# Hybrid decoder layer on one core: value products one slot later, score masks and weight splits ahead of the scan on VectorE

## Chip, core and metric

One core of a Trainium2 chip (trn2). The metric is the device time of one launch in microseconds (us), lower is better. All arithmetic is fp32; each large product is made of three passes in a reduced fp32 form.

## What is computed

One inference step of a one-layer hybrid decoder, for 256 prompt tokens and 8 sequences of 8 new tokens (320 tokens, model width 2048). Cut to what matters:

```python
z = rmsnorm(x) @ w_in                       # 2048 -> 5120
q, k, v, u, h, gb, gc = split(z)            # three mixers read z
o_att = dilated window attention(q, k, v)   # 16 heads of 64; sequences read 1280 of the 2048 cached rows each
y_ssm = complex diagonal scan over time(u), then GELU and a gated linear unit
y_conv = gb * conv3(gc * h)
mixed = concat(rmsnorm(o_att), rmsnorm(y_ssm), rmsnorm(y_conv))
x = x + mixed @ w_out
x = x + (silu(xn @ w_gate) * (xn @ w_up)) @ w_down
y = rmsnorm(x)
```

## The kernel before

**Tiles.** Features lie on the 128 partitions, the 320 tokens on the free axis. A weight *unit* is 128x1024 numbers (512 KB): two input tiles of 128 by 512 outputs. ScalarE (ACT) rounds a unit to its high part (`high`, L581, tile `whi`), VectorE (DVE) subtracts to get the low part (`low`, L886, `wlo`), and TensorE (PE) runs 24 matmuls of 320 columns on it (L1724 to L1726: high by high, high by low, low by high). `whi` and `wlo` have two buffers, so unit s+2 is split after PE has finished unit s and before it begins unit s+2.

**Slots.** The program up to the last third of the output projection is written as 96 slots. In slot s, PE runs unit s; `middle(s)` puts other matmuls after half of its unit, `end(s)` puts more behind it. Units 0 to 79 are the input projection, 80 and later the output projection. Each engine has its own hand-written order over the slots, and constants say which slot holds what:

- `START_OF[b]` is the first slot of sequence b; the sequences are six slots apart. In steps 0 to 4 PE makes the scores (`scores`, L1532) and DVE masks them out of bank 6 (`mask_scores`, L919); in step 4 ACT takes the exponent (L604); in step 5 PE turns the first two pieces of the probabilities (L1551), in step 6 the third, and ACT copies them out (L612); in steps 6 to 10 PE multiplies by the cached values (`values`, L1558), and in step 11 turns the result (L1581). Sequences 0 and 1 are finished late, in `LATE_SLOTS`.
- The scan runs over 16 groups of states, five parts each (`scan`, L936 to L958), all on DVE, spread over slots 24 to 65. Before a group, PE projects it in a `middle` (L1505, banks 6 and 7) and ACT copies it out (L687); GpSimd (POOL) makes the table of the group's powers. Part 0 of a group waits for both.
- The attention of the prompt runs over 8 pairs of heads from slot `PROMPT0`: scores (L1590), masks on DVE (L975), exponents, `prompt_norms` on DVE (L986), turning on PE (L1605), product (L1616).
- Three of the five norms lie in the slots: the input norm (its sum on PE in slot 8, its chain on DVE in slots 9 and 10: L853, L857 to L859), that of the scan's output (`SUM_SSM`: sum L1488, root on ACT, chain, `normed` L991) and that of the convolution (`SUM_CONV`).
- In DVE's slot come, in this order: two evictions (in every eighth slot, later every second), variance, `prompt_norms`, `prompt_masks`, those scan parts up to the last part 0 of the slot, two evictions, `mask_scores`, `low(s + 2)`, other work, and the remaining scan parts.

**Transfers.** All are issued by the SyncE queue (SP), in program order: the unit five slots ahead, then the cache pieces (512 KB each) of the slot. Each score step takes two pieces, each value step two; they share a ring of `KV` = 7 buffers, and a piece is issued when the one seven places ahead of it has been used.

**After the slots** PE runs the rest of the output projection and the feed-forward layer in loops (L1779 to L1781, L1828 to L1830), where nothing is changed. At the end the squares of the last tiles are added, the scale is spread over the partitions, DVE scales 12 output tiles (L1262) and POOL four (L1477), two tiles at a time, and SP stores them.

## Time and profile before

| | us |
|---|---|
| median of 3 runs | 1553.22 (1550.26 to 1553.37) |
| the profiled execution | 1552.25 |
| its span, first to last instruction | 1550.4 |
| PE busy | 1508.8 |
| DVE busy | 818.3 |
| ACT busy | 572.4 |
| POOL busy | 266.2 |

The profiled execution is 1.0 us under the median, and its span 1.85 us under its own time. PE is busy in the records when any matmul runs; a matmul's record is longer than the distance to the next one. The granted TensorE clock is 0.993 of full speed on average over the span.

### The profile page before, as it was taken

What the parts mean: (1) busy time and instruction counts of PE and PEld (TensorE: products, weight loads), DVE (VectorE), ACT (ScalarE), POOL (GpSimd) and SP (SyncE); (2) the same over time, 40 slices, a digit from 0 to 9 for tenths busy, and PEclk for the clock granted to TensorE, in tenths of its full rate; (3) what the DMA queues carried; (4) which work ended last, traced back from release to release, by engine and by line L of the source; (5) the groups of instructions that cost most, each with busy time, mean ns of one, the idle gap of its engine ahead of it and who ended that gap; (6) DMA issues with size and microseconds to landing.
All of it is one profiled execution on the core that took longest, in us unless ns stands there. A gap on an engine that the chain in (4) does not pass through costs nothing.

```text
span 1550.4 us, 27086 instructions
## 1 busy us (share of the span) xinstructions
PE 1508.8 (97%) x11084; PEld 1422.2 (92%) x11084; DVE 818.3 (53%) x1063; ACT 572.4 (37%) x751; POOL 266.2 (17%) x371
## 2 busy tenths in 40 slices
PE   9999999999989999999999999999999999999997
PEld 8998777667777899999999999999999999999997
DVE  6668987674264767544444444444444433333334
ACT  6333332225554435333333333333333333333332
POOL 7986655420170000000000000000000000000100
PEclk9999999999999999999999999999999999999998
DMA  7545799989669544444444444444444444444442
GB/s 257 186 158 196 258 361 349 360 321 343 249 230 391 165 139 149 149 150 149 149 149 149 149 149 149 149 148 150 149 148 150 148 150 150 150 148 152 148 151 107
DMA packets 82994, 296.59 MB, mean 191 GB/s; under 512 B 9952, under 2 KB 10848, under 8 KB 82528
## 3 DMA queue, kind: packets, MB, share of 16 engines
q1 hardware_dynamic: 82912, 295.43, 55.8%
q8 instruction: 60, 0.98, 0.3%
q14 instruction: 22, 0.18, 0.0%
HBM read 289.31 MB, written 5.43 MB: 190 GB/s over the span
## 4 chain that ended last, share of the span: by engine, by line
PE 82%; DVE 6%; issue 6%; DMA 4%; ACT 1%; POOL 1%; SPq 0%; POOLq 0%; ACTq 0%; DVEq 0%
PE ps L1829 18%; PE ps L1828 18%; PE ps L1830 18%; PE ps L1724 6%; PE ps L1726 5%; PE ps L1725 5%; DMA kv<-in_cv 3%; PE ps L1532 2%; PE ps L1558 2%; DVE wlo L886 1%; PE ps L1781 1%; PE ps L1780 1%; PE ps L1779 1%; DVE tm L937 1%; PE ps L1505 1%
## 5 line engine op out<-in xcount | busy, mean ns | idle before, releaser
L1151 DVE TENSOR_TENSOR wlo<-raw,whi 128x1024 fp32r<-128x1024 f32 x264 | 325.2, 1232 | 519.9 <-ACT whi L768 519.8
L768 ACT ACTIVATE whi<-raw 128x1024 fp32r<-128x1024 f32 x264 | 279.9, 1060 | 606.2 <-PE ps L1830 601.7
L1830 PE MATMUL ps<-xh,wlo 128*128 128x320 f32 x1400 | 432.8, 309 | 0.0
L1828 PE MATMUL ps<-xh,whi 128*128 128x320 f32 x1400 | 432.8, 309 | 0.0
L1829 PE MATMUL ps<-xl,whi 128*128 128x320 f32 x1400 | 432.7, 309 | 0.0
L1828 PEld LDWEIGHTS ps<-xh,whi 128*128 128x128 f32 x1400 | 262.8, 188 | 0.0
L1829 PEld LDWEIGHTS ps<-xl,whi 128*128 128x128 f32 x1400 | 262.8, 188 | 0.0
L1830 PEld LDWEIGHTS ps<-xh,wlo 128*128 128x128 f32 x1400 | 262.8, 188 | 0.0
L1724 PE MATMUL ps<-xh,whi 128*128 128x320 f32 x760 | 246.1, 324 | 9.2 <-DVE wlo L886 6.1
L1726 PE MATMUL ps<-xh,wlo 128*128 128x320 f32 x760 | 235.8, 310 | 0.0
L1725 PE MATMUL ps<-xl,whi 128*128 128x320 f32 x760 | 235.7, 310 | 0.0
L1830 PE MATMUL ps<-hh,wlo 128*128 128x320 f32 x696 | 215.2, 309 | 0.0
L1828 PE MATMUL ps<-hh,whi 128*128 128x320 f32 x696 | 215.2, 309 | 0.0
L1829 PE MATMUL ps<-hl,whi 128*128 128x320 f32 x696 | 215.1, 309 | 0.0
L581 ACT ACTIVATE whi<-raw 128x1024 fp32r<-128x1024 f32 x111 | 117.5, 1059 | 242.6 <-PE ps L1726 213.6
L886 DVE TENSOR_TENSOR wlo<-raw,whi 128x1024 fp32r<-128x1024 f32 x111 | 143.3, 1292 | 88.7 <-ACT whi L581 88.5
L1468 POOL TENSOR_TENSOR sq_last<-sq_last 128x1280 f32<-128x1280 f32 x2 | 5.9, 2970 | 1006.2 <-ACT sq_last L562 1006.2
L1724 PEld LDWEIGHTS ps<-xh,whi 128*128 128x128 f32 x760 | 143.6, 189 | 35.5 <-issue 25.7
L1725 PEld LDWEIGHTS ps<-xl,whi 128*128 128x128 f32 x760 | 143.8, 189 | 0.6
L1726 PEld LDWEIGHTS ps<-xh,wlo 128*128 128x128 f32 x760 | 143.6, 189 | 0.0
L1830 PEld LDWEIGHTS ps<-hh,wlo 128*128 128x128 f32 x696 | 130.7, 188 | 0.0
L1829 PEld LDWEIGHTS ps<-hl,whi 128*128 128x128 f32 x696 | 130.7, 188 | 0.0
(301 smaller groups left out, 1502.9 us busy)
## 6 DMA issues: line engine op xcount, KB each, us to landing
raw<-in_w_gu SPq DMA_DIRECT2D x176, 512.0 KB, 3.4
raw<-in_w_dn SPq DMA_DIRECT2D x88, 512.0 KB, 3.4
kv<-in_ck SPq DMA_DIRECT2D x80, 512.0 KB, 7.6
kv<-in_cv SPq DMA_DIRECT2D x80, 512.0 KB, 7.8
raw<-in_w_in SPq DMA_DIRECT2D x79, 512.0 KB, 4.9
raw<-in_w_out SPq DMA_DIRECT2D x32, 512.0 KB, 3.5
out_kv<-z SPq DMA_DIRECT2D x2, 1280.0 KB, 9.9
x<-in_xt SPq DMA_DIRECT2D x4, 640.0 KB, 9.8
```

The costliest lines, as they stand in the source:

```text
L581: act.activation(whi[:, u % SPL, :], raw[:, u % RAW, :], ACT.Copy).then_inc(S["w_hi"], 1)
L768: act.activation(whi[:, j % SPL, :], raw[:, j % RAW, :], ACT.Copy).then_inc(S["w_hi"], 1)
L886: v.tensor_tensor(wlo[:, u % SPL, :], raw[:, u % RAW, :], whi[:, u % SPL, :].bitcast(F32), ALU.subtract) \
L1151: v.tensor_tensor(wlo[:, j % SPL, :], raw[:, j % RAW, :], whi[:, j % SPL, :].bitcast(F32), ALU.subtract) \
L1532: last = t_.matmul(ps[32 * c:32 * c + 32, 6, cols], qst[:, b % 2, 2 * c + half, :], keys(2 * c + half), start=(half == 0), stop=(half == 1 ...
L1558: last = t_.matmul(ps[32 * c:32 * c + 32, bank, 0:2 * P], turned[:, 32 * c:32 * c + 32], vals[:, 2 * P * c:2 * P * c + 2 * P], start=start ...
L1724: t_.matmul(out, whi[:, u % SPL, w], xh[:, k, :], start=first, stop=False)
L1725: t_.matmul(out, whi[:, u % SPL, w], xl[:, k, :], start=False, stop=False)
L1726: last = t_.matmul(out, wlo[:, u % SPL, w], xh[:, k, :], start=False, stop=final)
L1828: t_.matmul(out, whi[:, slot, w], ah[:, k, :], start=(k == 0), stop=False)
L1829: t_.matmul(out, whi[:, slot, w], al[:, k, :], start=False, stop=False)
L1830: last = t_.matmul(out, wlo[:, slot, w], ah[:, k, :], start=False, stop=(k == 2 * units - 1))
```

## The change

- `START_OF` begins one slot earlier for every sequence. Scores, exponents and turned probabilities come a slot earlier; the value products are now steps 7 to 11, so they keep their slots, and the result is turned in step 12, also the same slot. In `end(s)` PE makes values before it turns probabilities. The pieces in the ring are ordered accordingly: two in the first score slot, four in each of the next four, two in the slot of the last values.
- On DVE no scan part stands ahead of the late evictions, masks and split any more: all parts of a slot come last. The 62 later parts are spread over 28 slots instead of 29.
- The prompt's attention, the gated unit and the norm of the scan's output come one slot earlier; the late products of sequences 0 and 1 in slots 57 and 61 instead of 58 and 60.
- The input norm's chain takes slots 9, 10 and 11, and the evictions behind it slots 12 to 14. The scan norm's chain takes two slots.
- DVE adds the four tiles of squares of the second and third norm in two operations, and PE makes one matmul of the sum instead of four.
- The first two x tiles and the first weight unit are loaded whole. Four reloads of x are issued apart instead of two by two.
- The output is scaled in nine pieces, the first two on DVE of one tile.

```diff
-LATE_SLOTS = (58, 60)
+LATE_SLOTS = (57, 61)
-SCAN0, SCAN1, SCAN_END, SCAN_FIRST = 24, 37, 66, 18
-PROMPT0 = 67
-SUM_SSM, SUM_CONV = 77, 84
+SCAN0, SCAN1, SCAN_END, SCAN_FIRST = 24, 37, 65, 18
+PROMPT0 = 66
+SUM_SSM, SUM_CONV = 76, 84
-START_OF = (37, 43, 49, 55, 61, 67, 73, 79)
+START_OF = (36, 42, 48, 54, 60, 66, 72, 78)
+TURN, VALUES, OUTPUT = 5, 7, 12
-SAMPLE_SLOT = START_OF[-1] + 12
+SAMPLE_SLOT = START_OF[-1] + OUTPUT + 1
...
+        Y_DVE = ((4, 1), (5, 1), (6, 2), (8, 2), (10, 2), (12, 2), (14, 2))
+        Y_POOL = ((0, 2), (2, 2))
...
-            here += [("v", b, j, 0) for b in range(DEC_BATCH) for j in range(KEY_TILES) if START_OF[b] + 6 + j // 2 == s]
+            here += [("v", b, j, 0) for b in range(DEC_BATCH) for j in range(KEY_TILES) if START_OF[b] + VALUES + j // 2 == s]
...
                 if s == N_IN:
...
-                    for c in range(2):
-                        sy.dma_start(x1[:, 4 * c:4 * c + 4, :], a["xt"][:, 4 * c:4 * c + 4, :]).then_inc(S[f"x_back{c}"], 16)
+                    load_x(0)
+                if s == N_IN + 2:
+                    load_x(1)
...
-            for kk in range(2):
-                sy.dma_start(x1[:, kk, :], a["xt"][:, kk, :]).then_inc(S[("x_first", "x_in0")[kk]], 16)
-                half = slice(512 * kk, 512 * kk + 512)
-                sy.dma_start(raw[:, 0, half], weight(0)[:, half]).then_inc((S["raw_first"], RAW_IN[0])[kk], 16)
-            for j in range(1, U_IN):
+            for j in range(U_IN):
                 sy.dma_start(x1[:, 2 * j:2 * j + 2, :], a["xt"][:, 2 * j:2 * j + 2, :]).then_inc(S[f"x_in{j}"], 16)
                 if j < RAW:
                     unit(j)
...
-                parts = scan_parts(s)
-                starts = [n for n, (_, part) in enumerate(parts) if part == 0]
-                early_parts = starts[-1] + 1 if starts else 0
-                for i, part in parts[:early_parts]:
-                    scan(i, part)
                 if is_last(s) and s >= 2 * U_IN - 1:
                     evict(s, 2)
                     evict(s, 3)
...
                 if s == 10:
-                    scales_rest(0, rstd)
+                    rstd_step(v.tensor_tensor(rtmp[:], rstd[:], rstd[:], ALU.mult))
+                if s == 11:
...
-                if 11 <= s < 15:
-                    evict(U_IN - 1, s - 11)
+                if s in (12, 13, 14):
+                    for n in ((0,), (1,), (2, 3))[s - 12]:
+                        evict(U_IN - 1, n)
...
+                for n, (at, src) in enumerate(((SUM_SSM - 1, sqs), (SUM_CONV - 1, sqc))):
+                    if s == at:
+                        dve.wait_ge(S["sq_ready"], 5 + n)
+                        step(v.tensor_tensor(src[:, 0:2], src[:, 2:4], src[:, 0:2], ALU.add))
+                        v.tensor_tensor(src[:, 0], src[:, 1], src[:, 0], ALU.add).then_inc(S["sq_paired"], 1)
...
                 if s == SUM_SSM:
-                    scales(1, rstd_s)
+                    scales_first(1, rstd_s)
+                if s == SUM_SSM + 1:
+                    scales_rest(1, rstd_s)
                     normed(ZU, V_OUT + 12, rstd_s)
-                for i, part in parts[early_parts:]:
+                for i, part in scan_parts(s):
                     scan(i, part)
...
-                    sums(sqs, range(NC), 5)
+                    sums(sqs, [0], 5)
...
-                for b in batches(s, 5):
-                    turn_probabilities(b, 0)
-                    turn_probabilities(b, 1)
                 for step in range(KN):
                     for b in batches(s, step):
                         scores(b, step)
-                for step in range(6, 11):
-                    for b in batches(s, step):
-                        values(b, 2 * step - 12)
-                        values(b, 2 * step - 11)
+                for j in range(0, KEY_TILES, 2):
+                    for b in batches(s, VALUES + j // 2):
+                        values(b, j)
+                        values(b, j + 1)
+                for b in batches(s, TURN):
+                    turn_probabilities(b, 0)
+                    turn_probabilities(b, 1)
```

The order that results, at three places. **DVE in slots 26 and 27** (`tm` and `hb` are scan tiles, `wlo` the split; before, lines L886 and L936; now L892 and L942), before:

```order
L886 TENSOR_TENSOR wlo<-raw,whi 128x1024
L949 TENSOR_TENSOR tm<-tm,tab 128x640
L950 TENSOR_TENSOR tm<-tm,tab 128x640
L955 TENSOR_TENSOR hb<-tm 128x320
L956 TENSOR_TENSOR hb<-tm 128x320
L958 COPY ho<-hb 128x2x9
L936 TENSOR_TENSOR tm<-xs,tab 128x640
L937 TENSOR_TENSOR tm<-xs,tab 128x640
L886 TENSOR_TENSOR wlo<-raw,whi 128x1024 x2
```

Now:

```order
L892 TENSOR_TENSOR wlo<-raw,whi 128x1024
L955 TENSOR_TENSOR tm<-tm,tab 128x640
L956 TENSOR_TENSOR tm<-tm,tab 128x640
L961 TENSOR_TENSOR hb<-tm 128x320
L962 TENSOR_TENSOR hb<-tm 128x320
L964 COPY ho<-hb 128x2x9
L892 TENSOR_TENSOR wlo<-raw,whi 128x1024
L942 TENSOR_TENSOR tm<-xs,tab 128x640
L943 TENSOR_TENSOR tm<-xs,tab 128x640
```

The split of unit 29 stood behind part 0 of the next group and now stands ahead of it.

**DVE in slots 55 and 56**, from the four evictions of slot 55 to the mask of slot 56, on which PE's turning of the new values in slot 56 waits. Before, the split stands behind a mask (not shown), and nine scan operations follow it:

```order
L886 TENSOR_TENSOR wlo<-raw,whi 128x1024
L945 SCALAR_TENSOR_TENSOR tm<-dec,tm 128x320
L946 SCALAR_TENSOR_TENSOR tm<-dec,tm 128x320
L949 TENSOR_TENSOR tm<-tm,tab 128x640
L950 TENSOR_TENSOR tm<-tm,tab 128x640
L955 TENSOR_TENSOR hb_odd<-tm 128x320
L956 TENSOR_TENSOR hb_odd<-tm 128x320
L958 COPY ho<-hb_odd 128x2x9
L936 TENSOR_TENSOR tm<-xs,tab 128x640
L937 TENSOR_TENSOR tm<-xs,tab 128x640
L919 ISA sall,smax<-ps,mask 128x256
```

Now:

```order
L892 TENSOR_TENSOR wlo<-raw,whi 128x1024
L955 TENSOR_TENSOR tm<-tm,tab 128x640
L956 TENSOR_TENSOR tm<-tm,tab 128x640
L961 TENSOR_TENSOR hb_odd<-tm 128x320
L962 TENSOR_TENSOR hb_odd<-tm 128x320
L964 COPY ho<-hb_odd 128x2x9
L942 TENSOR_TENSOR tm<-xs,tab 128x640
L943 TENSOR_TENSOR tm<-xs,tab 128x640
L925 ISA sall,smax<-ps,mask 128x256
```

Seven scan operations stand between that split and that mask instead of nine; the two of part 2 (L951, L952) have moved ahead of the evictions.

**DVE around the second norm** (`rstd_s` is its scale, `sp` the prompt's probabilities, which PE waits for at L1605), before:

```order
L886 TENSOR_TENSOR wlo<-raw,whi 128x1024
L853 RECIPROCAL rstd_s<-rtmp 128x320
L857 TENSOR_TENSOR rtmp<-rstd_s 128x320
L858 SCALAR_TENSOR_TENSOR rtmp<-rtmp,var 128x320
L859 SCALAR_TENSOR_TENSOR rstd_s<-rtmp,rstd_s 128x320
L991 SCALAR_TENSOR_TENSOR z<-z,vec,rstd_s 128x320 x4
L982 RECIPROCAL pmax<-pmax 128x4
L986 TENSOR_SCALAR sp<-sp,pmax 128x128
```

Now:

```order
L859 RECIPROCAL rstd_s<-rtmp 128x320
L988 RECIPROCAL pmax<-pmax 128x4
L992 TENSOR_SCALAR sp<-sp,pmax 128x128
L992 TENSOR_SCALAR sp<-sp,pmax 128x256
L992 TENSOR_SCALAR sp<-sp,pmax 128x128
L992 TENSOR_SCALAR sp<-sp,pmax 128x256
L892 TENSOR_TENSOR wlo<-raw,whi 128x1024
L1113 RECIPROCAL rsum<-rsum 128x1
L863 TENSOR_TENSOR rtmp<-rstd_s 128x320
L864 SCALAR_TENSOR_TENSOR rtmp<-rtmp,var 128x320
L865 SCALAR_TENSOR_TENSOR rstd_s<-rtmp,rstd_s 128x320
L997 SCALAR_TENSOR_TENSOR z<-z,vec,rstd_s 128x320 x4
```

Only the reciprocal is left ahead of the prompt's norms; three steps and four multiplications stand behind them and behind the split.

## Rows read from the trace of the kernel before

**Rows 1.** The page's line of busy time by engine

```profile
PE 1508.8 (97%) x11084; PEld 1422.2 (92%) x11084; DVE 818.3 (53%) x1063; ACT 572.4 (37%) x751; POOL 266.2 (17%) x371
```

**Rows 2.** Windows: start:end, length, busy us per engine, PEclk, DMA share, GB/s

```profile
100.00:155.00 55.00, 51.48 (x337) 47.18 (x336) 46.60 (x59) 16.98 (x20) 35.31 (x36) 1.00 0.58 191
...
185.00:225.00 40.00, 38.51 (x359) 28.38 (x358) 35.31 (x61) 12.41 (x20) 27.20 (x27) 1.00 0.89 345
...
225.00:265.00 40.00, 36.98 (x353) 28.65 (x352) 28.25 (x51) 11.60 (x19) 19.51 (x19) 1.00 0.90 336
...
700.00:1500.00 800.00, 800.00 (x5456) 800.00 (x5455) 338.96 (x270) 273.35 (x264) 9.25 (x4) 1.00 0.46 149
```

**Rows 3.** Waits of PE over the whole span: total us, times, longest

```profile
PE ps L1558 <- DMA kv<-in_cv: 8.2, 8, 1.9
...
PE ps L1724 <- DVE wlo L886: 6.1, 4, 1.7
...
PE ps L1558 <- ACT ptk L612: 1.7, 1, 1.7
...
PE ps L1605 <- ACT ptk L612: 1.3, 1, 1.3
...
PE ps L1505 <- DVE smax L919: 1.0, 2, 0.5
...
PE ps L1551 <- ACT sall L604: 0.9, 1, 0.9
...
PE ps L1532 <- DVE pmax L975: 0.8, 1, 0.8
```

**Rows 4.** Timeline of PE: start, us, line, [idle before it <- releaser]

```profile
12.43 0.42 PE L1724 MATMUL ps<-xh,whi 128*128 128x320 f32 x1 [1.40 <-DVE wlo L886]
...
57.50 0.42 PE L1724 MATMUL ps<-xh,whi 128*128 128x320 f32 x1 [1.70 <-DVE wlo L886]
...
118.32 0.41 PE L1724 MATMUL ps<-xh,whi 128*128 128x320 f32 x1 [1.50 <-DVE wlo L886]
...
280.71 0.39 PE L1685 MATMUL ps<-ident,z 128*64 128x128 f32 x1 [2.41 <-DVE smax L919]
...
452.22 0.47 PE L1605 MATMUL ps<-ident,sp 128*128 128x128 f32 x1 [3.01 <-DVE sp L986]
...
506.63 0.39 PE L1724 MATMUL ps<-xh,whi 128*128 128x320 f32 x1 [1.30 <-issue]
```

**Rows 5.** Timeline of DVE, two pieces from 115 to 120 us

```profile
115.46 1.24 DVE L937 TENSOR_TENSOR tm<-xs,tab 128x640 f32<-128x640 f32 x1
...
116.63 3.20 DVE L886 TENSOR_TENSOR wlo<-raw,whi 128x1024 fp32r<-128x1024 f32 x2
```

**Rows 6.** Groups of DVE instructions: busy, mean ns | idle before

```profile
L945 DVE TENSOR_TENSOR_SCAN tm<-dec,tm 128x320 f32<-128x320 f32 x16 | 14.2, 885 | 0.5 <-DVE tm L942 0.2
```

**Rows 7.** Timeline of DVE: first norm's last step, and the split behind it

```profile
54.00 1.22 DVE L859 SCALAR_TENSOR_TENSOR rstd<-rtmp,rstd 128x320 f32<-128x320 f32 x1
...
55.26 2.19 DVE L886 TENSOR_TENSOR wlo<-raw,whi 128x1024 fp32r<-128x1024 f32 x1
```

**Rows 8.** Windows behind the gaps at 280.71 and 452.22

```profile
280.50:284.00 3.50, 3.29 (x15) 3.07 (x16) 1.28 (x3) 1.18 (x2) 3.42 (x7) 0.52 1.00 421
...
452.30:459.00 6.70, 6.70 (x31) 6.02 (x32) 3.43 (x9) 1.88 (x7) 5.46 (x10) 0.58 0.23 78
```

**Rows 9.** Timeline of PE: the second norm's sum, 4 matmuls of 2 passes

```profile
435.52 2.42 PE L1488 MATMUL ps<-sqs,ones 128*128 128x320 f32 x8
```

**Rows 10.** Timeline of ACT: the second half of the first weight unit

```profile
7.60 0.63 ACT L665 ACTIVATE whi<-raw 128x512 fp32r<-128x512 f32 x1 [1.07 <-DMA raw<-in_w_in]
```

**Rows 11.** Windows: a stretch of cache loads; the tail

```profile
246.00:253.00 7.00, 5.28 (x56) 4.29 (x56) 5.38 (x9) 1.06 (x1) 6.92 (x8) 1.00 1.03 411
...
1541.00:1550.40 9.40, 1.24 (x6) 1.05 (x5) 4.48 (x6) 0.44 (x1) 3.03 (x2) 0.50 0.73 279
```

**Rows 12.** DMA issues: KB each, median us from issue to landing

```profile
out_y<-yout SPq DMA_DIRECT2D x8, 320.0 KB, 2.6
```

79 lines of the change are left out of this document (42 added, 37 removed).

## Prediction, made before the changed kernel was run

> **What bounds it now.** I read the page's busy line first: TensorE is busy for 1508.8 of 1550.4 us [rows 1], so only what shortens or closes up its work counts. The table of windows says where: from 700 to 1500 us it is busy in all 800.00 us, while windows before 351 us miss 1.5 to 3.5 us each [rows 2]. The change leaves the loops alone, so whatever is won in the slots arrives whole at the end. Third, the waits of TensorE and the single gaps [rows 3, 4]: that is the list to be worked through. In the scan's stretch DVE is busy for 46.60 of 55 us [rows 2], close to a bound of its own. Fourth, the granted clock: behind the gaps of 2.41 and 3.01 us it is 0.52 for 3.50 us and 0.58 for 6.70 us [rows 8], a mix of the levels of 1.2 and 2.4 GHz. TensorE had stood still before both falls.
>
> **Startup: 1.5 us.** Unit 1 starts at 12.43 after 1.40 us of waiting [rows 4]; the second half of the first weight is there only for a copy at 7.60 [rows 10]. The same bytes now come in two transfers instead of four and SP issues two less. The first product must then wait for the whole unit, about where that copy starts. Nothing saved to 2.0 us; I take 1.5, since unit 1 waits longer than one copy.
>
> **First norm: 1.3 us.** Its three steps ran in one piece, the last 1.22 us, and the split behind them 2.19 us [rows 7]; TensorE waited 1.70 us at 57.50 [rows 4]. Now one step stands in slot 10, two in 11. Two steps of 1.22 beside a split that itself ran for up to 2.19 just exceed what a slot leaves, so 0.4 us may stay. Bounds 1.2 and 1.7.
>
> **Scan ahead of the split: 2.0 us.** Waits for `wlo` are 6.1 us in four [rows 3]: 1.40, 1.70, and 3.0 in two gaps like that at 118.32 [rows 4]. Part 0 of a group stood ahead of the split; its second operation alone took 1.24 us, and two splits followed it back to back [rows 5]. It now stands behind. But DVE does the same work in 46.60 of 55 us [rows 2]: at the eviction slots 31 and 39, TensorE arrives earlier at a bank that DVE has not emptied, and gives about 1 us back. Bounds 1.0 and 3.0. Projections wait 1.0 us for masks [rows 3]; masks go earlier where no third scan part is in the way: 0.5 us.
>
> **Cache pieces: 5.6 us.** Eight waits, 8.2 us [rows 3]. A slot with scores and values asks for five pieces, 2.62 MB, five slots running; now four slots running, with two lighter slots beside them. At the 411 GB/s of the stretch 246 to 253 us [rows 11], 2.62 MB take 6.4 us, near a slot's own time there, so the backlog grows with each slot, and a shorter run with a rest before it cuts the later waits. Two thirds of 8.2 go: 5.6. Bounds 2, if only one wait in four was the last of such a run, and 8.2.
> A rule speaks against this: the Trainium skill (DMA: Bandwidth & Descriptors, Bandwidth) puts the limit of HBM traffic of one core at about 358 GB/s. By it the stretch from 185 to 265 us, at 345 and 336 GB/s [rows 2], would already be at its limit, and this term would be about 2 instead of 5.6. The trace shows 411 [rows 11], above it, so I go by the trace; the case is part of the second rival.
>
> **The new values at 280.71: 0.9 and 1.7 us.** They wait 2.41 us for the mask of slot 56 [rows 4]. Nine scan operations stood ahead of that mask, seven now; the two that leave take about 2 x 0.85 us (a scan operation is 885 ns on average [rows 6]), and TensorE also arrives earlier, so about 1.5 us of wait stay. Then the clock should not fall: 3.50 us at 0.52 cost 3.50 x 0.48 = 1.7 us [rows 8]. Bounds for both together 0 and 4.1.
>
> **Late product: 1.7 us.** Sequence 1's late product shared slot 60 and bank 7 with turned probabilities and waited 1.7 us for ACT's copy [rows 3]. In slot 61 bank 7 has long been emptied. Bounds 1.2 and 1.7.
>
> **Second norm: 2.6 and 2.8 us.** PE waited 0.9 us for the exponent [rows 3] and 3.01 us for `sp` behind the whole chain [rows 4]. Now values cover the exponent, and only the reciprocal is ahead of `sp`. What is late next is bank 6: turned probabilities and the prompt's still meet in slot 77, as where 1.3 us were waited for ACT's copy [rows 3]. So 0.9 + 3.0 - 1.3 = 2.6. The clock at 0.58 for 6.70 us cost 2.8 us [rows 8]; 1.3 us is no gap behind which it fell. Bounds 3 and 6.7. The steps now follow in slot 77, behind its split; the next split is a whole slot away, which hides them. If DVE were late there, the masks of pair 6 would be next.
>
> **Sums: 3.2 us.** Four matmuls of two passes take 2.42 us [rows 9], the last pass some 0.2 us of overhang; three quarters of 2.2 go, 1.6 us, twice. DVE's four added operations lie in slots 75 and 83, where no scan is left. Bounds 2.8 and 3.6.
>
> **Smaller ones.** Prompt masks late by 0.8 us [rows 3] stood behind an eviction that waited for reloaded x; one reload is issued later, 0.6 us. At 506.63 TensorE waited 1.30 us [rows 4] for evictions behind the third norm's chain; this chain is whole still, one more operation of the attention follows it, and TensorE comes earlier by what its sum no longer takes, so 0.7 us *more*. Bounds -1.5 and 0. Tail: stores run at 279 GB/s over 9.40 us [rows 11], so they end earlier only as the first starts earlier; half of one two-tile multiplication (4.48 / 6 / 2) gives 0.4 us. The Trainium skill (the same page and section) lets transfers of 64 KB move at 138 and of 1 MB at 341 GB/s, so that splitting a 320 KB store costs rather than gives; by that the tail would be 0.2 us longer and the whole sum 0.6 less. Here 320 KB land in 2.6 us amid other stores [rows 12]; the term is too small for either to matter to the range.
>
> **Sum.** 1.5 + 1.3 + 2.0 + 0.5 + 5.6 + 0.9 + 1.7 + 1.7 + 2.6 + 2.8 + 3.2 + 0.6 - 0.7 + 0.4 = 24.1 us. Every engine's order is new over 60 slots, so waits that no row shows will appear; I allow three of 0.9 us, the size of the exponent's wait [rows 3]: 2.7. That leaves 21.4. The profiled execution, 1552.25, would become 1530.9; against the median of 1553.2, 1531.8.
>
> **Rivals.**
> *More is given back (0.30).* DVE and the transfers bound the scan's stage: no gain for splits, projections and the mask at 280.71 (2.0, 0.5, 0.9), 2 instead of 5.6 for the cache, the clock falls again there (1.7) and new waits take 3 more. That is 11.7 less: 1543.5. For it: 46.60 of 55 us on DVE and 345 GB/s [rows 2]. Against: DVE's busy share falls to 28.25 of 40 us later, and 411 GB/s.
> *All of it closes up (0.10).* No new waits, all cache waits and splits gone: 2.7 + 2.6 + 1.0 more, and 1 at the start: 1524.5.
> *The scan falls behind (0.05), slower.* With all parts last, part 0 of a group is done late in its slot; ACT must see it before it may copy the next projection out, and the high part of unit s+2 is queued behind that copy, and the split and TensorE behind it. It decides once DVE is later than a slot's second half plus the projection, some 3 us. If 13 groups of slots 37 to 65 then each wait for one part 0, about 2 us (0.9, a scan operation's mean [rows 6], and 1.24 [rows 5]), that is 26 us: 1558. Against: the windows from 185 to 265 us hold some six slots each, and DVE is busy in them for 35.31 and 28.25 us of 40 [rows 2].
> *It does not arrive (0.05).* The gaps closed in the slots open again before evictions, whose order is unchanged, as a bank can be taken only when DVE has emptied it: 1553, within 0.2%, which is about what a measurement of this kernel can tell from no change (3.1 us).
>
> **Numbers.** The forecast has 0.50 (1526 to 1538), the others as said. Faster by over 0.2%: 0.50 + 0.30 + 0.10 = 0.90; same 0.05; slower 0.05. The likeliest is 1531.8. The range reaches down to the third case, 1524.0, and up past the second's 1543.5, whose new waits may be larger by half, to 1546.0; outside lie the last two cases and the ends of these, under 2 in 10.
>
> **What would show it.** In the new profile: no wait of TensorE over 2 us in the slots, no window at a clock near 0.5 before the tail, two passes at the sums, DMA waits for values under 3 us in total, nothing over 0.5 us at the end of slots 12, 28 and 35, and a wait of about 2 us before slot 86. The start of the loops should be some 21 us earlier. Wrong would be: waits for `xs` or `wlo` at many slots from 37 to 65 (the slower rival), or the saving shrinking between slot 43 and slot 66 (the first).

## The result, and the profile after

| | before | after |
|---|---|---|
| median | 1553.3 us (1550.26 to 1554.12, 4 runs) | 1536.14 us (1534.52 to 1537.62, 4 runs) |
| the profiled execution | 1552.25 | 1536.85 |
| its span | 1550.4 | 1535.0 |
| granted TensorE clock, mean | 0.993 | 0.996 |

The ratio is 0.9893, 95% interval 0.9876 to 0.991: 16.6 us faster by this ratio, with 14.0 to 19.3 us inside the interval. The forecast was 21.4 us less (1531.8, range 1524.0 to 1546.0). Three executions further down, two of the kernel before and one of the old slot numbers, took 2455 us or more in a disturbed state, and all medians are taken without them.

The page's busy line of the changed kernel, beside [rows 1]:

```profile
PE 1504.5 (98%) x11072; PEld 1417.8 (92%) x11072; DVE 824.9 (54%) x1068; ACT 572.1 (37%) x751; POOL 264.6 (17%) x371
```

TensorE is busy for 4.3 us less. The rest of the 15.4 us between the spans was idle time.

The waits of PE over the whole span of the changed kernel (total us, times, longest), beside [rows 3]:

```profile
PE ps L1571 <- DMA kv<-in_cv: 5.3, 5, 2.1
PE ps L1737 <- issue: 3.5, 2, 2.7
PE ps L1737 <- DVE z L908: 2.7, 3, 1.4
PE ps L1618 <- DVE smax L925: 1.9, 1, 1.9
...
PE ps L1698 <- DVE smax L925: 1.7, 1, 1.7
PE ps L1564 <- ACT xs L693: 1.5, 1, 1.5
...
PE ps L1545 <- ACT xs L693: 0.9, 1, 0.9
PE ps L1737 <- DVE wlo L892: 0.9, 2, 0.7
PE ps L1618 <- ACT ptk L619: 0.8, 2, 0.4
```

Waits for `wlo` fell from 6.1 to 0.9 us, waits for `ptk` from 3.0 to 0.8, and those for `sp`, `sall` and `pmax` are gone. Cached values fell only from 8.2 to 5.3. Waits for late evictions (`z`, L908) grew from 0.5 to 2.7. Three kinds are new: for `xs` (2.4 us in two), for a score mask in front of the prompt's turning (L1618, 1.9 us), and a longer one at the output projection's eviction (L1737 <- issue).

The gaps one by one, from the timeline of PE of the changed kernel, beside [rows 4]:

```profile
107.64 0.41 PE L1737 MATMUL ps<-xh,whi 128*128 128x320 f32 x1 [0.72 <-DVE wlo L892]
...
127.85 0.38 PE L1737 MATMUL ps<-xh,whi 128*128 128x320 f32 x1 [1.42 <-DVE z L908]
...
177.93 0.74 PE L1564 MATMUL ps<-ident,sall 128*128 128x128 f32 x5 [1.46 <-ACT xs L693]
...
275.83 1.03 PE L1698 MATMUL ps<-ident,z 128*64 128x128 f32 x8 [1.67 <-DVE smax L925]
...
450.25 0.85 PE L1618 MATMUL ps<-ident,sp 128*128 128x128 f32 x6 [1.86 <-DVE smax L925]
...
490.31 0.38 PE L1737 MATMUL ps<-xh,whi 128*128 128x320 f32 x1 [2.67 <-issue]
```

The gap at 280.71 of before is the one at 275.83 here (2.41 to 1.67 us), that at 506.63 is now at 490.31 (1.30 to 2.67). The last two gaps stand behind these pieces of DVE's timeline, first slot 79, then slots 85 and 86:

```profile
447.29 0.87 DVE L908 TENSOR_TENSOR z<-ps,rstd 128x320 f32<-128x320 f32 x2
448.08 1.68 DVE L1004 TENSOR_TENSOR xl<-z,xh 128x320 fp32r<-128x320 f32 x4
449.69 0.41 DVE L925 CUSTOM_DVE_ANT_0 sall<-ps,mask 128x256 f32<-128x256 f32 x1
...
485.55 2.15 DVE L859 RECIPROCAL rstd<-rtmp 128x320 f32<-128x320 f32 x1 [0.56 <-ACT rtmp L573]
487.74 0.49 DVE L863 TENSOR_TENSOR rtmp<-rstd 128x320 f32<-128x320 f32 x1
488.26 0.49 DVE L864 SCALAR_TENSOR_TENSOR rtmp<-rtmp,var 128x320 f32<-128x320 f32 x1
488.79 0.49 DVE L865 SCALAR_TENSOR_TENSOR rstd<-rtmp,rstd 128x320 f32<-128x320 f32 x1
489.32 0.48 DVE L1009 SCALAR_TENSOR_TENSOR al<-z,vec,ah 128x256 fp32r<-128x256 f32 x1
489.72 1.68 DVE L913 TENSOR_TENSOR x<-ps,x 128x320 f32<-128x320 f32 x4
```

In slot 79 two evictions and four low parts of the gated tiles (L1004, `mixed_low`) stand ahead of the mask (L925) that clears bank 6, a bank of PSUM that TensorE needs next. In slot 86 the evictions stand behind 3.6 us of chain (2.15 + 3 x 0.49) and 0.48 of the attention.

The windows of the changed kernel (start:end, length, busy us per engine, PEclk, DMA share, GB/s), beside [rows 2, 8]:

```profile
185.00:225.00 40.00, 39.38 (x366) 29.55 (x365) 34.35 (x61) 12.45 (x20) 24.24 (x27) 1.00 0.92 346
225.00:265.00 40.00, 37.87 (x354) 28.27 (x353) 30.79 (x52) 12.44 (x20) 22.67 (x26) 1.00 0.91 341
...
491.00:494.70 3.70, 3.70 (x17) 3.70 (x17) 3.70 (x7) 0.00 (x0) 0.00 (x0) 0.54 0.55 187
700.00:1500.00 800.00, 800.00 (x5456) 800.00 (x5456) 338.66 (x269) 273.48 (x264) 9.26 (x4) 1.00 0.46 149
```

The loops are as they were. The two stretches at half clock [rows 8] are gone, and a new one stands behind the gap of slot 86; at 0.54 for 3.70 us it cost 3.70 x 0.46 = 1.7 us by the clock (1.3 to 1.5 by the time of its stage, as the last section shows).

By stages, from the first matmul of each slot in the two traces (us between them):

| stage | before | after | gain |
|---|---|---|---|
| start to slot 1 | 12.4 | 11.1 | 1.3 |
| slots 1 to 14 | 48.7 | 47.0 | 1.7 |
| slots 14 to 36 | 87.6 | 86.2 | 1.4 |
| slots 36 to 66 | 197.6 | 194.9 | 2.7 |
| slots 66 to 76 | 80.0 | 80.4 | -0.4 |
| slots 76 to 80 | 37.1 | 31.5 | 5.6 |
| slots 80 to 86 | 43.2 | 39.2 | 4.0 |
| slots 86 to 95 | 38.7 | 40.1 | -1.4 |
| slot 95 to the end | 1005.1 | 1004.7 | 0.4 |

The steps of the sequences lie one slot earlier, so the work of a stage is not quite the same in both. Still, the missing part is plain: for slots 36 to 66 the terms of the forecast came to 10.4 us (0.5 + 5.6 + 0.9 + 1.7 + 1.7), and 2.7 came.

The prediction had named signs to look for. Seen as named: two passes at the sums, and nothing over 0.5 us at the end of slots 12, 28 and 35. Not seen as named: TensorE waited over 2 us twice (2.67 in front of slot 86, where about 2 had been named, and 2.07 for a cached piece), one stretch near half clock came ahead of the tail, waits for values were 5.3 us instead of under 3, and the loops begin 14.9 us earlier instead of some 21. Of the two signs that it would be wrong, the saving did not shrink between slots 43 and 66 (2.3 us at slot 43, 7.1 at slot 66), and waits for `xs` came at two slots, not at many.

### The profile page after: what moved, and what is told of

Its sections match the earlier page's. It is cut to its first block, busy times and chain, and to the rows that moved or that the text cites. A ratio compares the mean times of both kernels' runs of the same rounds, so it can differ in the third digit from the quotient of the medians.

```text
span 1535.0 us, 27068 instructions
## 1 busy us (share of the span) xinstructions
PE 1504.5 (98%) x11072; PEld 1417.8 (92%) x11072; DVE 824.9 (54%) x1068; ACT 572.1 (37%) x751; POOL 264.6 (17%) x371
## 4 chain that ended last, share of the span: by engine, by line
PE 85%; DVE 6%; issue 5%; DMA 2%; ACT 1%; POOL 1%; POOLq 0%; ACTq 0%; DVEq 0%
PE ps L1842 19%; PE ps L1841 19%; PE ps L1843 19%; PE ps L1737 6%; PE ps L1739 6%; PE ps L1738 6%; DMA kv<-in_cv 2%; PE ps L1545 2%; PE ps L1571 2%; DVE wlo L892 1%; PE ps L1794 1%; PE ps L1793 1%; PE ps L1792 1%; PE ps L1637 1%; PE ps L1532 1%
## 5 line engine op out<-in xcount | busy, mean ns | idle before, releaser
L1737 PE MATMUL ps<-xh,whi 128*128 128x320 f32 x760 | 245.6, 323 | 7.1 <-issue 3.5
L892 DVE TENSOR_TENSOR wlo<-raw,whi 128x1024 fp32r<-128x1024 f32 x111 | 142.4, 1283 | 79.8 <-ACT whi L588 79.4
L1737 PEld LDWEIGHTS ps<-xh,whi 128*128 128x128 f32 x760 | 143.2, 188 | 32.4 <-issue 29.6
L1841 PEld LDWEIGHTS ps<-hh,whi 128*128 128x128 f32 x696 | 130.6, 188 | 0.0
```

The source lines that it names most:

```text
L892: v.tensor_tensor(wlo[:, u % SPL, :], raw[:, u % RAW, :], whi[:, u % SPL, :].bitcast(F32), ALU.subtract) \
L1737: t_.matmul(out, whi[:, u % SPL, w], xh[:, k, :], start=first, stop=False)
L1841: t_.matmul(out, whi[:, slot, w], ah[:, k, :], start=(k == 0), stop=False)
```

## Experiments

Each is the changed kernel with one edit, unless said otherwise. Old slot numbers, scan early, third norm spread and mask first ran on one chip (before: 1550.4 us there); these two together, four sums, short values and second norm whole on another (1549.2); the changed kernel again, the old slot numbers again, half units and five places mended on a third (1550.5). Since cached pieces come later or earlier from one execution to the next, and stretches at half clock come and go, the trace is read beside the times in one table (all from the profiled execution; "falls" are the stretches at half clock ahead of the tail, with their lengths in us):

| kernel | median, us | ratio, 95% | slot 95 begins | waits for cached values | slot 95 less these | falls |
|---|---|---|---|---|---|---|
| before | 1553.3 | 1 | 545.3 | 8.2 | 537.1 | 3.4, 6.8 |
| after | 1536.1 | 0.9893 [0.9876, 0.991] | 530.4 | 5.3 | 525.1 | 3.4 |
| after, again | 1534.9 | 0.9902 [0.9885, 0.9919] | 527.8 | 2.8 | 525.0 | 3.4 |
| old slot numbers | 1538.8 | 0.993 [0.9913, 0.9946] | 528.0 | 5.4 | 522.6 | 3.4 |
| the same, again | 1540.4 | 0.9927 [0.9904, 0.995] | 535.8 | 7.7 | 528.1 | 3.4, 3.4, 3.4 |
| scan early | 1536.3 | 0.9913 [0.9894, 0.9931] | 529.7 | 3.6 | 526.1 | 3.4 |
| third norm spread | 1532.5 | 0.9887 [0.9871, 0.9904] | 524.5 | 2.7 | 521.8 | none |
| mask first | 1533.2 | 0.9887 [0.9871, 0.9904] | 527.6 | 2.4 | 525.2 | 6.8 |
| these two | 1531.9 | 0.9889 [0.9874, 0.9905] | 524.8 | 4.0 | 520.8 | none |
| four sums | 1536.4 | 0.9915 [0.9901, 0.9929] | 531.6 | 4.1 | 527.5 | 3.4 |
| short values | 1531.0 | 0.9881 [0.9866, 0.9897] | 524.7 | 0 | 524.7 | 3.4 |
| second norm whole | 1537.7 | 0.9924 [0.991, 0.9939] | 534.7 | 5.8 | 528.9 | 3.4, 3.4 |
| half units | 1536.7 | 0.9911 [0.9895, 0.9927] | 529.9 | 2.6 | 527.3 | 6.8 |
| five places mended | 1527.4 | 0.9853 [0.9834, 0.9872] | 521.3 | 3.3 | 518.0 | none |

The column "less these" agrees to 0.1 us between the two executions of the changed kernel, whose slot 95 began 2.6 us apart. That is closer than it can be trusted: single stages of the two still differ by up to 0.6 us and happen to cancel, and the two executions of the old slot numbers differ by 5.5 in this column, of which the two further stretches at half clock explain 3.4. Differences of single edits are therefore read from the stage that the edit touches. The ratios cannot carry them alone: those of third norm, mask first and both (0.9887 to 0.9889) lie 0.6 to 2.3 us under the two of the changed kernel (0.9893 and 0.9902), well inside each other's intervals.

**The slot numbers.** All parts of the change stay, in the old slots:

```diff
-LATE_SLOTS = (57, 61)
+LATE_SLOTS = (58, 60)
-SCAN0, SCAN1, SCAN_END, SCAN_FIRST = 24, 37, 65, 18
-PROMPT0 = 66
-SUM_SSM, SUM_CONV = 76, 84
+SCAN0, SCAN1, SCAN_END, SCAN_FIRST = 24, 37, 66, 18
+PROMPT0 = 67
+SUM_SSM, SUM_CONV = 77, 84
-START_OF = (36, 42, 48, 54, 60, 66, 72, 78)
-TURN, VALUES, OUTPUT = 5, 7, 12
+START_OF = (37, 43, 49, 55, 61, 67, 73, 79)
+TURN, VALUES, OUTPUT = 5, 6, 11
```

> The changed kernel with the slot numbers of the kernel before (values in steps 6 to 10, scan end, prompt, second norm and late products back in their slots); the orders inside a slot, the two norm chains, the paired sums, startup and tail stay changed. Theory A (each closed gap is won by its own part of the change): the numbers carry the late product (1.7 us) and the shorter cache waits (8.2 to 5.3, so 2.9 us), but also cost the 1.4 us longer gap before slot 86 and its fall of the clock (1.7 us), so this kernel takes 1537 to 1540 us, waits for cache pieces come back to about 8 us and no clock near 0.5 is seen in the slots. Theory B (the numbers carry nearly all, the order inside the slots nothing): 1546 us or more.

Measured 1538.79 us (1535.19 to 1540.93), ratio 0.993: slower than the changed kernel, as the first theory said, but not in the way it said: in this profile the waits for cached values were 5.4 us, not 8, and a stretch at half clock was there (at 439.5 us) that it had ruled out. So it was run once more, beside the changed kernel.

> The changed kernel itself, unchanged, on the same chip and against the same runs of the kernel before as the next three. Its ratio was 0.9893 [0.9876, 0.991]. Theory A (ratios of different chips can be compared to 0.1%): 0.988 to 0.9905, 16 to 17 us saved. Theory B (the kernel before differs from chip to chip by the luck of its cache loads, and the ratio moves with it): outside of that.

1534.91 us (1533.89 to 1537.49), ratio 0.9902: the ratios on the two chips agree to 0.1%, as the first theory had it, though 15.2 us saved are a little under its 16 to 17.

> The changed kernel with the old slot numbers once more (sequences, prompt, scan end, norm and late products where they were, the order of values and turned probabilities and all other parts as changed), beside the changed kernel on one chip. Theory A (the new slot numbers are worth what the first ratios say, 0.993 against 0.9893): 4 to 7 us slower than the changed kernel, mainly by longer waits for cached values. Theory B (they are worth what the two profiles say, in which slot 95 began at 528.0 with the old numbers and at 530.4 us with the new): within 2 us of the changed kernel, so that the gain comes from the order inside the slots, the norms, the sums and the start.

1540.40 us is the median (1536.24 to 1543.10): 5.5 us slower than the changed kernel, ratio 0.9927 against 0.9902. The first theory holds, though the two intervals overlap a little (0.9904 to 0.995, and 0.9885 to 0.9919); the first pair of ratios says the same. From the waits of PE and its timeline in this run:

```profile
PE ps L1571 <- DMA kv<-in_cv: 7.7, 7, 2.9
...
286.34 0.64 PE L1571 MATMUL ps<-kv,ptk 128*32 128x256 f32 x8 [2.95 <-DMA kv<-in_cv]
```

And the three stretches at half clock that are in it, as windows:

```profile
250.20:253.60 3.40, 3.40 (x15) 2.35 (x15) 2.58 (x3) 0.00 (x0) 2.54 (x4) 0.50 1.03 412
287.70:291.20 3.50, 3.50 (x15) 2.24 (x15) 0.00 (x0) 0.00 (x0) 1.03 (x1) 0.51 1.03 408
311.60:315.00 3.40, 3.40 (x15) 3.40 (x15) 2.30 (x5) 0.00 (x0) 1.09 (x2) 0.51 0.33 117
```

Two of them follow a late cached piece (2.95 us at 286.34, 1.91 us at 248.86) and one the late product, which waits 1.69 us for `ptk` again. In the three profiles with the old numbers (before among them) cached values are waited for 8.2, 5.4 and 7.7 us, mean 7.1. In the ten with the new numbers and whole pieces it is 2.4 to 5.8, mean 3.7. So the new numbers take off some 3.4 us of waiting and, in some executions, the falls behind it. But with the old numbers slot 86 waited 1.30 instead of 2.67 us and the mask of slot 79 not at all: the new numbers brought both of these. The edit puts the late products back with the sequences, so it does not tell their shares apart.

**Scan parts ahead of masks and split again.**

```diff
+                parts = scan_parts(s)
+                starts = [n for n, (_, part) in enumerate(parts) if part == 0]
+                early_parts = starts[-1] + 1 if starts else 0
+                for i, part in parts[:early_parts]:
+                    scan(i, part)
                 if is_last(s) and s >= 2 * U_IN - 1:
...
-                for i, part in scan_parts(s):
+                for i, part in parts[early_parts:]:
```

> The changed kernel with the scan parts up to the last part 0 of a slot again ahead of the late evictions, masks and split. Theory A: the gaps of 1.5 us for splits before slots 29 and 36 and the long wait for the mask in slot 56 (over 2.4 us, with the clock down for 3.4 us) come back, 5.4 us, and the waits for the copy of a projection in slots 41 and 61 (1.46 and 0.89 us) and some of the other new ones go, so 1538 to 1540 us. Theory B (DVE's work bounds the stage, so its order only moves the gaps): 1535 to 1537 us, and slot 66 starts within 1 us of the changed kernel's.

1536.28 us (1534.89 to 1539.46), and 526.1 against 525.0 in the table: the second theory's time holds, and the first's 1538 to 1540 does not. From the timeline of PE of this kernel, the old waits are back and one is new:

```profile
116.92 0.42 PE L1742 MATMUL ps<-xh,whi 128*128 128x320 f32 x1 [1.78 <-DVE wlo L892]
...
147.34 0.41 PE L1742 MATMUL ps<-xh,whi 128*128 128x320 f32 x1 [1.49 <-DVE wlo L892]
...
273.77 0.41 PE L1742 MATMUL ps<-xh,whi 128*128 128x320 f32 x1 [2.56 <-DVE z L908]
```

Slots 14 to 36 take 88.9 us here against 86.2 and 86.6 in the two executions of the changed kernel, so there the new order is worth 2.3 to 2.7. Slots 36 to 66, less their waits for cached values, take 188.4 against 190.4 and 189.8: there it costs 1.4 to 2.0, because the waits for `xs` come with it. The order is a gain in the first half of the scan and a loss in the second. The reason that the second theory gave, that DVE's work bounds the stage, is not what this shows: the last experiment below does the same work in less time.

**The third norm's chain spread over two slots.**

```diff
                 if s == SUM_CONV:
-                    scales(2)
+                    scales_first(2)
                 if s == SUM_CONV + 1:
+                    scales_rest(2, rstd)
                     normed(ZH, V_OUT, rstd)
```

> The changed kernel with the third norm's chain spread as the second's: only the reciprocal in its slot, the three steps in the next one behind the split. Theory A (the gap of 2.67 us before slot 86 is this chain ahead of the evictions, and the clock fell because of it): the gap shrinks to 1 us or less, the clock stays up, 1532 to 1533 us. Rival (the chain is only late somewhere else: the normed tiles, and PE waits for them at slot 88): 1536 us, with a new gap of about 2 us at slot 88.

1532.54 us (1531.67 to 1533.58), and 3.2 us less in the table. The timeline of PE has

```profile
485.71 0.38 PE L1738 MATMUL ps<-xh,whi 128*128 128x320 f32 x1 [1.09 <-issue]
```

and no stretch at half clock in the slots. Slots 80 to 86 take 37.6 us instead of 39.2, slots 86 to 95 take 38.8 instead of 40.1: 1.6 us of gap and 1.3 of clock, as the first theory had it.

**The mask of slot 79 ahead of the low parts.**

```diff
-                if s == N_IN - 1:
-                    mixed_low(ZU, 12, KT)
                 for step_ in range(KN):
                     for b in batches(s, step_):
                         mask_scores(b, step_)
+                if s == N_IN - 1:
+                    mixed_low(ZU, 12, KT)
```

> The changed kernel with the score mask of slot 79 ahead of the four low parts of the scan's output. Theory A (the 1.86 us before the prompt's turning in slot 79 is the mask behind these four): the gap goes, 1534 to 1534.5 us. Rival (cache pieces or the reloads of x bound the next slots): the 1.86 us come back as waits for transfers by slot 83, 1536 us.

1533.16 us (1532.48 to 1534.02). The gap of 1.86 us is gone, and slots 76 to 80 take 29.9 us instead of 31.5. But the stretch at half clock behind the gap of slot 86 was 6.8 us long in this profile instead of 3.4 (slots 86 to 95 take 41.3 instead of 40.1), and slot 1 began 0.6 us later, so the table shows nothing (525.2). Both edits together:

> The changed kernel with two edits together: the third norm's chain spread over slots 84 and 85, and in slot 79 the mask of the last sequence's scores ahead of the four low parts of the gated tiles. Theory A (gaps are independent, and each stands on what DVE has in line ahead of the operation that TensorE waits for): the wait of 1.86 us at slot 79 and about 1.6 of the 2.67 us at slot 86 go, together with the stretch at half clock that cost 1.7 us; in the slots no granted clock near 0.5 is left; span 4 to 5.5 us under that of the changed kernel, 1530.5 to 1532. Theory B (an engine that is freed at one place gives it back at the next): the two edits together give no more than the larger alone, 1532.5 to 1534.

1531.91 us (1530.41 to 1534.04), span 1530.2. The trace is as the first theory had it: slots 76 to 80, 80 to 86 and 86 to 95 take 29.9, 37.7 and 38.8 us, each as in the run of its own edit, with no fall. The gap of 1.86 us is gone, that of slot 86 is down to 1.09. The median is only 0.6 us below that of the third norm's edit alone, on another chip, and the ratios are the same (0.9889 and 0.9887), so the times by themselves do not show that the second edit adds anything.

**The sums as four matmuls again** (L1656 and L1660 back to `sums(sqs, range(NC), 5)` and `sums(sqc, range(NC), 5)`, DVE's four additions left out).

> The changed kernel with the sums of the second and third norm made again by four matmuls over the four tiles of squares, and without DVE's four additions. Theory A (the term of the sum was right: three of four matmuls of two passes each fall away, twice): TensorE is busy 3.2 us longer and the time rises by 2.8 to 3.6 us, to 1539 to 1540. Theory B (the matmuls filled time in which TensorE would have waited for evictions or for the split): the time rises by under 1 us.

1536.35 us (1534.78 to 1538.70). TensorE is busy for 1508.4 us instead of 1504.5 and 1505.0. Timeline of PE, this kernel's sum (the changed kernel's takes 0.81 us, in two passes) and the wait of slot 79:

```profile
423.11 2.42 PE L1496 MATMUL ps<-sqs,ones 128*128 128x320 f32 x8
...
451.92 0.85 PE L1613 MATMUL ps<-ident,sp 128*128 128x128 f32 x6 [0.93 <-DVE smax L925]
```

The term is right: 2.42 - 0.81 = 1.6 us, twice. But the first 1.6 us shorten the wait for the mask of slot 79 by 0.93 (from 1.86), so the kernel loses 2.4 us by the table, between the two theories (2.0 of them in slots 76 to 86, where the sums are). In the changed kernel 0.9 of the sums' 3.2 us ran into that wait.

**Short pieces of values.** 256 of 1024 columns are loaded of each piece of cached values after the first seven, so the attention's output is computed from incomplete values:

```diff
-                sy.dma_start(kv[:, n % KV, :], src).then_inc(KV_IN[n % KV], 16)
+                if kind == "v" and n >= KV:
+                    sy.dma_start(kv[:, n % KV, 0:256], src[:, 0:256]).then_inc(KV_IN[n % KV], 16)
+                else:
+                    sy.dma_start(kv[:, n % KV, :], src).then_inc(KV_IN[n % KV], 16)
```

> The changed kernel, but the cached pieces of values after the first seven load only 256 of their 1024 columns, so part of the attention's input is left out; count and order of the transfers are the same. Theory A (what is left of the waits for cached values, 5.3 us in five, is the rate of the transfers, and nothing else stands behind it): those waits go, the time falls by 4 to 5.3 us, to 1531 to 1532. Theory B (the stage of slots 36 to 65 is bound by DVE as well, which would be late next): the waits for values go, but waits for evictions, masks or the copy of the projection take over more than half of it; the time falls by 2 us or less.

1531.04 us (1530.01 to 1531.51). By the ratio, 0.9881, that is 1.9 to 3.3 us less than the changed kernel; the 4 to 5.3 us of the first theory were counted from one profile with many such waits. No wait for values is left, the other large gaps of the stage are where they were and within 0.1 us as long, and the table gives 524.7 against 525.1 and 525.0. The windows:

```profile
185.00:225.00 40.00, 39.38 (x366) 29.52 (x366) 34.34 (x62) 12.46 (x20) 24.71 (x28) 1.00 0.73 245
225.00:265.00 40.00, 39.99 (x373) 30.70 (x373) 33.52 (x57) 12.45 (x20) 22.67 (x26) 1.00 0.81 260
```

At 245 and 260 instead of 346 and 341 GB/s, DVE does as much and is not late more often. So the waits for cached values add to the time as they stand, and DVE is not what held them up: the first theory.

**The second norm's chain in one piece, ahead of the prompt's norms.**

```diff
                 if s == SUM_SSM:
-                    scales_first(1, rstd_s)
-                if s == SUM_SSM + 1:
-                    scales_rest(1, rstd_s)
+                    scales(1, rstd_s)
                     normed(ZU, V_OUT + 12, rstd_s)
```

> The changed kernel with the second norm's chain and its four multiplications again in one piece in slot 76, ahead of the prompt's norms of that slot. Theory A (the two largest terms of the sum are due to this edit alone): TensorE waits about 2.5 to 3 us for sp at slot 77 or 78 and runs at half clock for 3.4 to 6.8 us behind it; the time rises by 4 to 5.5 us, to 1540 to 1542. Theory B (the move by one slot and the changed order of values and turned probabilities already cover the chain): the wait is under 1.5 us, no fall of the clock, the time rises by 1.5 us or less.

1537.71 us (1537.28 to 1541.83), ratio 0.9924 against 0.9893 and 0.9902: 3.4 to 4.8 us. Timeline of PE:

```profile
440.14 1.11 PE L1616 MATMUL ps<-ident,sp 128*128 128x128 f32 x4 [3.04 <-DVE sp L992]
```

A stretch of 3.4 us at half clock begins at 439.9, and the mask of slot 79 is waited for 0.93 us less: 3.0 + 1.7 - 0.9 = 3.8. Slots 76 to 80, where all of this lies, take 34.5 us instead of 31.5: 3.0, and not all of 3.8. The table also shows 528.9 - 525.1 = 3.8, but by chance: slot 1 began 1.2 us later in this profile, one more stretch at half clock stands at 286.3 behind a wait for a cached piece, and the one behind slot 86 is missing. First theory by the wait and the clock; the time rose by less than its 4 to 5.5 us.

**Start with half units** (two tiles of x and two halves of the first weight unit, each with its own transfer and semaphore, as before).

> The changed kernel with the first two x tiles and the first weight unit loaded in two halves each again, on SP, ACT and DVE as before. Theory A (the startup term of the sum): unit 1 starts at 12.4 instead of 11.1 us and the time rises by 1.3 to 1.5 us. Theory B (the first wait of unit 1 comes from the second unit's own load, which varies from run to run): unit 1 starts at 11.4 or earlier, no difference.

1536.74 us (1535.26 to 1537.49), 1.8 us slower than the changed kernel on the same chip. Unit 1 starts at 12.37 us; in the changed kernel at 11.11 and 11.67. First theory; 0.7 to 1.3 us of it are the start itself, and the stretch at half clock was 6.8 us long in this profile. The second theory is not wholly out: over the twelve profiles here with the first unit loaded whole, unit 1 starts at 11.10 to 12.34 us, 11.5 in the mean, against 12.43 and 12.37 in the two with halves. So the term is worth some 0.9 us on average, and one execution in twelve had next to nothing of it.

**Five places mended.** To the two edits above come: part 0 ahead of masks and split in slots 40 and 60 alone, the last part of group 1 in slot 31, part 0 of group 12 in slot 56.

```diff
+SCAN_LATER = {(1, 4): 31, (12, 0): 56}
...
+            if (i, part) in SCAN_LATER:
+                return SCAN_LATER[i, part]
...
+                starts = [n for n, (_, part) in enumerate(parts) if part == 0 and s in (40, 60)]
```

> The changed kernel with the third norm's chain spread, the mask of slot 79 ahead of the low parts, part 0 of the scan ahead of masks and split in slots 40 and 60 alone, the last part of group 1 in slot 31 instead of 30, and part 0 of group 12 (with its projection) one slot later, in 56. Theory A (every gap is closed by its own edit): beside the kernel with the first two edits, whose slot 95 began at 524.8 us, the waits of 1.46 us at slot 41 and 0.89 at slot 61 go, that of 1.51 at slot 32 falls under 0.8, that of 1.67 at slot 56 falls under 0.5; slot 95 begins 3 to 4.5 us earlier and the time is 1527 to 1529. Theory B (DVE is near its bound there and each of these only moves the wait): slot 66 begins within 1.5 us of where it did, 1530 to 1532.

1527.41 us (1526.42 to 1530.03), ratio 0.9853 [0.9834, 0.9872] against the kernel before, and 7.5 us less than the changed kernel on the same chip: faster than both. First theory. The waits for `xs` at slots 41 and 61 and that for the mask at slot 56 are under 0.5 us, that of slot 32 is 0.50. Two new gaps, in the timeline of PE:

```profile
174.48 0.81 PE L1527 MATMUL ps<-z,bt 32*128 32x320 f32 x4 [1.10 <-DVE smax L933]
...
473.83 0.51 PE L1510 MATMUL ps<-sqc,ones 128*128 128x320 f32 x1 [1.27 <-DVE sqc L1089]
```

The first is the price of part 0 in slot 40: its two operations, 2.1 us, now stand ahead of that mask. The second was 0.3 us; the additions stood behind evictions that waited for reloaded x, as TensorE now arrives earlier there.

## Why the forecast was right, and where it was not

**Right in size.** Startup: 1.5 forecast, 1.3 and 0.8 in the two profiles of the changed kernel, some 0.9 over all profiles. First norm: 1.3, and slots 1 to 14 gained 1.7. Late product: 1.7, gone in the new profile and back as 1.69 us with the old numbers. Second norm: 2.6 of waiting; the piece taken apart removes 3.0 of waiting, of which 0.9 came back at slot 79. Its clock: 2.8 forecast from 6.70 us at 0.58; undone, the piece brought a stretch of 3.4 us back, 1.7. Sums: 3.2 forecast, 3.2 measured on the engine, of which 0.9 is hidden in the changed kernel. Prompt masks: the 0.8 us are gone. Wait at 280.71: 0.9 forecast, 0.7 came (1.1 in the second profile), and the clock no longer falls there. Tail: 0.4 forecast, 0.4 in one profile and -0.2 in the other, too small to be told from nothing. The first norm, the late product's slot, the reloads of x and the tail were undone by no run of their own; these terms rest on the waits that are gone from the trace.

**Cache pieces: mis-sized.** The term said that two thirds of 8.2 us go, 5.6. In the profile compared, 2.9 went; over ten profiles with the new numbers the mean left is 3.7, so about 3.4 to 4.5 go. The mechanism fits: fewer pieces in a row, and less waiting in the mean; that the waits are the transfers' own is shown by the short pieces, while the backlog itself was tested by no run. What the step missed is that the wait is no fixed quantity of the kernel: the same code gave 5.3 and 2.8. The bounds of 2 and 8.2 held it. As to the limit of about 358 GB/s in the Trainium skill (DMA: Bandwidth & Descriptors, Bandwidth): two of the windows above, of the old slot numbers, run at 412 and 408. The same page, in its table of measured transfers, has one core alone at 425 GB/s for a transfer of 16 MB and calls about 358 the share of a core when both of a pair stream; this case, with one core, agrees with that.

**Slot 86: wrong in a cause and in its consequence.** The step was "0.7 us *more*" for the wait in front of it; it became 1.4 us more (1.30 to 2.67). Of its three causes the shorter sum is none. With the old slot numbers and one matmul for the sum the wait is 1.30 us as before, and with the new numbers and four matmuls it is 2.66: DVE's chain starts behind the sum and moves with it. Timelines of PE and DVE from that sum on, with the old slot numbers and then in the changed kernel:

```profile
479.50 0.70 PE L1501 MATMUL ps<-sqc,ones 128*128 128x320 f32 x2
...
487.00 1.07 PE L1571 MATMUL ps<-kv,ptk 128*32 128x256 f32 x16
...
488.78 1.68 DVE L913 TENSOR_TENSOR x<-ps,x 128x320 f32<-128x320 f32 x4
```

```profile
480.04 0.78 PE L1501 MATMUL ps<-sqc,ones 128*128 128x320 f32 x2 [0.28 <-DVE sqc L1081]
...
486.57 1.07 PE L1571 MATMUL ps<-kv,ptk 128*32 128x256 f32 x16
```

From the start of the sum the evictions begin after 9.28 us and, in the changed kernel, after 9.68 (489.72): the attention's operation costs 0.4. TensorE is through after 8.57 us and now after 7.60, as less turning of probabilities stands in slots 84 and 85 than with the old numbers: 1.0. Together these are the 1.4, and the step had the first of them but not the second. It also did not ask whether a gap of that length brings half clock, though [rows 8] showed a fall behind 2.41 us: another 1.3 to 1.7. The edit that spread this third chain takes the fall away and 1.6 us of the gap.

**The scan ahead of the split: right, and then not.** 2.0 and 0.5 us were claimed for the whole scan. Undoing it costs 2.3 to 2.7 us in slots 14 to 36 and gives 1.4 to 2.0 in slots 36 to 66. The chain that brings this was described, under the slower rival: part 0 last, ACT's copy of the next projection behind it, and its readers behind that. The rival expected the high part of the weights to be the victim, at 13 groups; it was at two places, and its victims were turned probabilities and scores, since bank 6 is not free until the copy is done. ACT's timeline at slot 41 of the changed kernel:

```profile
177.08 0.70 ACT L693 ACTIVATE xs<-ps 128x640 f32<-128x640 f32 x1 [2.24 <-DVE tm L943]
```

So that rival was right in kind and wrong by a factor of ten in its size: 26 us at 13 groups, against 2.4 us at two places.

**The allowance for new waits: too small.** Three of 0.9 us were allowed, 2.7. Late evictions and splits came at slot 27 (0.72 us), 32 (0.9 more than before), 40 (0.63) and 48 (0.62), of which the scan's term had set 1 aside; beside them 1.46 us at slot 41, 0.89 at slot 61, and 1.86 at slot 79. The largest could have been read from the order beforehand: four low parts of 0.42 us each and two evictions ahead of a mask, in a slot where the mask is now awaited, since the prompt's probabilities are turned in odd slots instead of even ones.

**The sum.** The forecast had 13.7 us of waiting less and 7.7 us less of matmuls (sums 3.2, clock 1.7 and 2.8); the traces have 11.1 and 4.3. The waiting, against the terms: cache 2.7 short, slot 86 0.7, the scan's order 1.9, new waits 1.5 beyond the allowance, the mask at 280.71 0.2, together 7.0. More than forecast went of the waits for ACT's copies of `ptk` in the prompt (1.8: two of 1.3 were expected to stay or come, 0.34 and 0.41 are there), of a score's wait for a mask that no term had (0.9), of the masks ahead of projections (0.5), of the start (0.6), the first norm (0.4) and the prompt's masks (0.2), together 4.4. That makes the 2.6 between 13.7 and 11.1. It is luck that the total came so near: 7.0 us fell short, and 4.4 came from places where the forecast had not put them. Of the matmuls' 3.4 us, 1.7 are the new stretch at half clock. For the rest, take the time that TensorE is busy between the starts of slots 1 and 95, less half of what of it ran at half clock:

| kernel | busy | at half clock | busy less half of that |
|---|---|---|---|
| before | 504.6 | 9.0 | 500.1 |
| old slot numbers | 498.0 | 3.4 | 496.3 |
| the same, again | 501.6 | 10.2 | 496.5 |
| after | 499.9 | 3.4 | 498.2 |
| after, again | 499.9 | 2.9 | 498.4 |

From before to the old slot numbers 3.6 to 3.8 us go, of which the sums are 3.2, so the two old stretches did cost about what half clock says. From there to the changed kernel 1.7 to 2.2 us come back: with the new slot numbers the same matmuls keep TensorE busy for longer. The forecast put this at nothing, and no run shows which matmuls it is. Ahead of slot 1 TensorE is busy for 0.8 us more: the 32 matmuls on ones, with which it begins, took 6.42 us in the changed kernel's profile and 5.19 before. With the 1.7 of the new stretch that is 4.2 to 4.7; the tail took 0.4 less, and 0.4 to 0.6 went beyond the sums, which closes the account.

**The rival of more given back**, 1543.5, had DVE and the transfers bound the stage. The short pieces speak against the DVE half of it: with the transfers light, DVE kept up. So do the five places: with the same scan work on DVE in another order, slots 36 to 66, less their waits for cached values, take 187.1 us, against 190.4 and 189.8.

## What to carry over

When one engine's list is reordered, go through every slot and ask, for each operation that moved down, who is waiting for it in *that* slot. A rule applied to all slots (all scan parts last) gained 2.3 to 2.7 us in one stage and lost 1.4 to 2.0 in another, while the same rule with two exceptions and two parts moved kept both. And a wait behind a transfer that runs near its rate is a distribution: before trusting a median to 2 us, take these waits and the stretches at half clock out, and compare the stage that the edit touches; a single total can agree by chance, as two did here.

## What was not expected of the hardware

**Half clock is not set by the length of one gap.** Windows of three kernels, the first behind the gap of 2.66 us at slot 86 of the kernel with four sums, the second behind 2.56 us in the kernel with the early scan, the third behind gaps of 0.70 and 1.02 us at 437.10 and 439.21 us with the old slot numbers:

```profile
493.00:496.50 3.50, 3.45 (x24) 3.48 (x24) 3.50 (x7) 0.00 (x0) 0.00 (x0) 1.00 0.49 171
```

```profile
273.80:277.30 3.50, 3.50 (x44) 2.67 (x44) 2.68 (x7) 1.06 (x1) 3.42 (x6) 1.00 1.02 423
```

```profile
439.40:443.00 3.60, 3.60 (x17) 3.42 (x16) 3.50 (x8) 2.04 (x8) 3.04 (x7) 0.53 0.46 151
```

TensorE stood at 2.4 GHz (1.00) behind the two long gaps and near 1.2 GHz (0.53) behind the two short ones. The gap of 2.67 us at slot 86 is in eight profiles (2.66 in one of them): six times a fall followed, of 3.4 us four times and of 6.8 twice, and twice none. Falls followed single gaps of 1.69 to 3.04 us, and none followed in other places 2.43, 2.07 or the 1.86 at slot 79. What a fall costs can be read off directly, since slots 86 to 95 ran behind the same gap in different ways: 38.5 us without a fall (four sums, second norm whole), 39.8 to 40.1 with 3.4 us of half clock, 41.3 with 6.8. So it is 1.3 to 1.5 or 2.7 to 2.8 us; part of such a stretch can lie in the gap itself, where it costs nothing. Closing a gap of 1 to 3 us is therefore worth its length, and this much more in some executions.

**The loads' rate.** 423 GB/s over 3.50 us in the second window is hardly above the 421 over 3.50 us of [rows 8], and above the 411 over 7 us of [rows 11].
